# The recurrent mixer's projections in another order, four buffers of split weights, gating scale and bias on VectorE, second output factor inside the solve

## What is computed

```python
p = rmsnorm(x, ev_norm) @ ev_w_in            # columns: u 512, va 512, r 512, k 512, v 512, lora 256
# gating half
vn = (va - mean) * rsqrt(var + eps) * ln_g + ln_b
y_a = u * (einsum('gts,bnsgc->bntgc', w_s * causal, vn) + b_s)
# recurrent half: r, k, v, lora parts are mixed with the row before
p = p + (shift_prev(p) - p) * mu
w, a, g = decay(lw), sigmoid(a0 + la @ a2), sigmoid(lg) @ g2
kk = normalised(k * k_k);  k = k * (1 + (a - 1) * k_a)
S = S * w + (S @ -kk) (kk * a)^T + v k^T;  o = S @ r      # over 256 steps
out = (norm(o) * gn_g + gn_b + sum(r * k * r_k) * v) * g
x = x + concat(y_a, out) @ ev_w_out
```

## Time and profile before

| | us |
|---|---|
| median of three runs | 1414.9 (1414.65 to 1417.06) |
| the profiled execution | 1414.84 |
| its span | 1413.0 |
| mean granted clock of TensorE | 0.976 |

### The profile page before, as it was taken

One profiled execution on the slowest core, in us unless ns is written; L12 is line 12 of the kernel. 1 busy time (PEld: TensorE's weight loads), 2 busy tenths in 40 slices (PEclk: granted clock), 3 DMA queues, 4 the chain that ended last, 5 costly groups with the idle time before them and its releaser, 6 DMA issues.

```text
span 1413.0 us, 24106 instructions
## 1 busy us (share of the span) xinstructions
PE 1333.2 (94%) x10315; PEld 1211.0 (86%) x10315; DVE 955.3 (68%) x1237; ACT 684.2 (48%) x974; POOL 22.6 (2%) x30
## 2 busy tenths in 40 slices
...
GB/s 292 142 119 61 4 120 209 238 239 239 241 177 180 178 61 60 265 194 262 252 248 135 177 122 119 60 350 328 339 305 260 132 224 179 123 208 198 188 179 60
DMA packets 161284, 263.78 MB, mean 187 GB/s; under 512 B 3533, under 2 KB 95897, under 8 KB 161178
## 3 DMA queue, kind: packets, MB, share of 16 engines
...
## 4 chain that ended last, share of the span: by engine, by line
PE 74%; DVE 12%; ACT 7%; issue 5%; DMA 2%; POOL 0%; SPq 0%; DVEq 0%; ACTq 0%; POOLq 0%
PE ps L867 22%; PE ps L840 13%; PE ps L841 13%; PE ps L842 13%; ACT whi L522 2%; PE ps L1968 2%; DVE wlo L528 2%; DVE acc L1846 2%; DMA ring<-in_ff_w_up_dram 1%; PE ps L2264 1%; DVE arena L1793 1%; PE ps L853 1%; PE ps L854 1%; PE ps L855 1%; DVE arena L1814 1%
## 5 line engine op out<-in xcount | busy, mean ns | idle before, releaser
L528 DVE TENSOR_TENSOR wlo<-ring,whi 128x2048 fp32r<-128x2048 f32 x195 | 445.6, 2289 | 227.4 <-ACT whi L522 227.1
L840 PE MATMUL ps<-ghi,whi 128*128 128x256 f32 x1856 | 521.9, 281 | 9.0 <-DVE glo L776 6.9
L841 PE MATMUL ps<-glo,whi 128*128 128x256 f32 x1856 | 517.6, 279 | 0.0
L842 PE MATMUL ps<-ghi,wlo 128*128 128x256 f32 x1856 | 517.1, 279 | 0.0
L522 ACT ACTIVATE whi<-ring 128x2048 fp32r<-128x2048 f32 x195 | 370.9, 1911 | 87.6 <-PE ps L867 68.0
L840 PEld LDWEIGHTS ps<-ghi,whi 128*128 128x128 f32 x1856 | 348.6, 188 | 15.8 <-issue 12.8
L841 PEld LDWEIGHTS ps<-glo,whi 128*128 128x128 f32 x1856 | 347.9, 187 | 1.0 <-issue 0.7
L842 PEld LDWEIGHTS ps<-ghi,wlo 128*128 128x128 f32 x1856 | 348.2, 188 | 0.0
L867 PE MATMUL ps<-whi,yhi 128*128 128x512 f32 x480 | 154.7, 404 | 5.0 <-DVE wlo L528 3.7
L867 PE MATMUL ps<-wlo,yhi 128*128 128x512 f32 x480 | 150.4, 395 | 0.0
L867 PE MATMUL ps<-whi,ylo 128*128 128x512 f32 x480 | 149.8, 394 | 0.0
...
## 6 DMA issues: line engine op xcount, KB each, us to landing
...
```

What stands on the lines that cost most here:

```text
L528: e.tensor_tensor(shaped(WLO[i % NB], k), v, shaped(WHI[i % NB], k).bitcast(F32), ALU.subtract).then_inc(S["w_lo"], 1)
L840: e.matmul(o, wh, h[0][:, k, :], start=k == 0, stop=False)
L841: e.matmul(o, wh, h[1][:, k, :], start=False, stop=False)
L842: x = e.matmul(o, wl, h[0][:, k, :], start=False, stop=k == NK - 1)
```

## The change

Five parts. The projections' order is `lora`, `k`, `va`, `r`, `u`, `v`; the banks' order and the queues of all five engines follow. `NB` is 4 and every stream is one half further ahead; a scratch area that nothing uses is made smaller for it. The gating half's gain and bias move from GpSimd to VectorE, into two fused operations per half that take the place of one; the gating's bias is one product of 512 columns per bank in place of one per block. `P2` moves into the second round of the solve. The column transposes and `rk` sums lie between `v 0` and `v 1`.

```diff
@@ -19,7 +19,7 @@
 NF = FF // 128
 NS = 2
 SLOT = 4096
-NB = 3
+NB = 4
 HALF = 2048
 KAPPA = float(np.exp(-0.5))
...
     w_in = A["ev_w_in"][0]
     chunks.append(("lora", cols_of(w_in, [2560], 256)))
-    for name, s in (("k", 1536), ("r", 1024), ("v", 2048), ("va", 512), ("u", 0)):
+    for name, s in (("k", 1536), ("va", 512), ("r", 1024), ("u", 0), ("v", 2048)):
         chunks.append((name, cols_of(w_in, [s], 512)))
     add_out("ev_out", A["ev_w_out"][0])
...
@@ -249,13 +249,11 @@
     r = Ring(range(6))
     P.use(("col", 6), r())
     norm(0, r, False)
-    for key in [("col", 0), ("lora", 0), ("k", 0), ("k", 1), *(("sg", w, q) for q, w in TWO), ("r", 0),
-                ("nm", 0), ("nm", 1), ("g", 0), ("g", 1), ("r", 1), ("v", 0), ("v", 1),
-                *(("col", t) for t in range(1, 6))]:
-        P.use(key, r())
     P.use(("va", 0), 6)
     P.use(("va", 1), 7)
-    for key in [("rk", 0), ("rk", 1), ("vt", 0), ("vt", 1), "ws", ("u", 0), ("ya", 0), ("ya", 1), ("u", 1)]:
+    for key in [("col", 0), ("lora", 0), ("k", 0), ("k", 1), *(("sg", w, q) for q, w in TWO), ("nm", 0), ("nm", 1),
+                ("g", 0), ("g", 1), ("r", 0), ("r", 1), "ws", ("u", 0), ("ya", 0), ("ya", 1), ("u", 1), ("v", 0),
+                *(("col", t) for t in range(1, 6)), ("rk", 0), ("rk", 1), ("v", 1), ("vt", 0), ("vt", 1)]:
         P.use(key, r())
     r = Ring(range(8))
...
@@ -500,13 +498,15 @@
             for off, k, w, src in chunks[n][1]:
                 e.dma_start(c3(ring[n % NS][:, off:off + k * w], k), src).then_inc(S[f"ring{n % NS}"], 16)
+        AHEAD = NB - 1
+
         class Stream:
             def __init__(self):
                 self.made, self.taken = 0, 0
-            def go(self, ahead=2):
+            def go(self, ahead=NB - 1):
                 self.taken += 1
...
@@ -1018,14 +1018,7 @@
             for n in range(2):
                 eye(flat64(Yb[1][n]), S["y_eye"])
-            e.wait_ge(S["ln_in"], 64)
-            for n in range(2):
-                e.wait_ge(*read_out(("va", n)))
-                e.tensor_tensor(VN[n], VN[n], LNG, ALU.mult).then_inc(S["vn_gain"], 1)
-                e.wait_ge(S["vn_gain"], n + 1)
-                e.tensor_tensor(VN[n], VN[n], LNB, ALU.add).then_inc(S["vn"], 1)
-
-            e.wait_ge(*used_up("u", 1))
+            e.wait_ge(*used_up("v", 1))
             for x in AKm:
...
             exps((0, 1))
             exps((2, 3))
+            for q in range(2):
+                t = TMP[:, 2 * q:2 * q + 2, :]
+                e.wait_ge(*read_out(("nm", q)))
+                e.activation(t, t, ACT.Ln).then_inc(S["kk_log"], 1)
+                e.wait_ge(S["kk_log"], q + 1)
+                e.activation(t, t, ACT.Exp, scale=-0.5).then_inc(S["kk_rstd"], 1)
             split_hi(e, w.go())
-            mixed(5)
+            for q in range(2):
+                e.wait_ge(S["g_mm"], q + 1)
+                for a in range(2):
+                    j = 2 * q + a
+                    ps = ps_of(("g", q))[:, 256 * a:256 * a + 256]
+                    e.activation(P1[:, j, :], ps, ACT.Copy, scale=cc("ev_gn_g", j))
+                e.activation(GATE[:, 2 * q:2 * q + 2, :], c3(ps_of(("g", q))[:, :], 2),
+                             ACT.Copy).then_inc(bank_sem(("g", q)), 1)
             e.wait_ge(S["e2"], 1)
             e.activation(E1, E2, ACT.Exp, scale=KAPPA).then_inc(S["s0_scale"], 1)
-            split_hi(e, w.go())
-            mixed(6)
-            split_hi(e, w.go())
             for n in range(2):
                 q = mv[:, 4 * n:4 * n + 4]
                 e.wait_ge(S["va_mean"], n + 1)
                 e.activation(q[:, 2:3], q[:, 1:2], ACT.Ln, bias=LN_EPS).then_inc(S["va_log"], 1)
                 e.wait_ge(S["va_log"], n + 1)
                 e.activation(q[:, 3:4], q[:, 2:3], ACT.Exp, scale=-0.5).then_inc(S["va_rstd"], 1)
-            for n in range(2):
-                e.wait_ge(S["v_turned"], n + 1)
-                e.activation(VT[:, n, :], ps_of(("vt", n))[:, :], ACT.Copy).then_inc(bank_sem(("vt", n)), 1)
+            split_hi(e, w.go())
+            mixed(3)
+            split_hi(e, w.go())
+            mixed(4)
             split_hi(e, w.go())
             for q in range(2):
                 e.wait_ge(S["ya_mm"], q + 1)
-                e.wait_ge(S["vn"], 2)
                 e.activation(MX[:, 2 * q:2 * q + 2, :], c3(ps_of(("ya", q))[:, :], 2),
                              ACT.Copy).then_inc(bank_sem(("ya", q)), 1)
             split_hi(e, w.go())
             for q in range(2):
                 e.wait_ge(*read_out(("u", q)))
                 e.activation(YT[0][:, 2 * q:2 * q + 2, :], MX[:, 2 * q:2 * q + 2, :], ACT.Copy).then_inc(S["ya_hi"], 1)
-                if q == 0:
-                    split_hi(e, w.go())
+            split_hi(e, w.go())
+            mixed(5)
+            split_hi(e, w.go())
+            mixed(6)
+            for n in range(2):
+                e.wait_ge(S["v_turned"], n + 1)
+                e.activation(VT[:, n, :], ps_of(("vt", n))[:, :], ACT.Copy).then_inc(bank_sem(("vt", n)), 1)
...
@@ -1479,6 +1468,35 @@
             x.then_inc(S["k_factor"], 1)
             e.wait_ge(S["k_factor"], 1)
             e.scalar_tensor_tensor(Km[:, :, :], TMP[:, :, :], 1.0, Km[:, :, :], ALU.add, ALU.mult).then_inc(S["k"], 1)
+            split_lo(e, w.go())
+            for n in range(2):
+                s6, q = st6[:, 6 * n:6 * n + 6], mv[:, 4 * n:4 * n + 4]
+                e.wait_ge(*used_up("va", 1))
+                e.bn_stats(s6, ps_of(("va", n))[:, :]).then_inc(S["va_stats"], 1)
+                e.wait_ge(S["va_stats"], n + 1)
+                e.bn_aggr(q[:, 0:2], s6).then_inc(S["va_mean"], 1)
+            e.tensor_tensor(Am[:, :, :], KKm[:, :, :], Am[:, :, :], ALU.mult).then_inc(S["b"], 1)
+            e.wait_ge(S["ln_in"], 64)
+            for n in range(2):
+                q, key = mv[:, 4 * n:4 * n + 4], ("va", n)
+                e.wait_ge(S["va_rstd"], n + 1)
+                e.wait_ge(S["g_mm"], 2)
+                e.scalar_tensor_tensor(VN[n], ps_of(key)[:, :], q[:, 0:1], LNG, ALU.subtract,
+                                       ALU.mult).then_inc(bank_sem(key), 1)
+                e.wait_ge(*read_out(key))
+                e.scalar_tensor_tensor(VN[n], VN[n], q[:, 3:4], LNB, ALU.mult, ALU.add).then_inc(S["vn"], 1)
+            split_lo(e, w.go())
+            e.wait_ge(S["ws_turned"], 1)
+            e.tensor_tensor(c3(WS, 4), c3(ps_of("ws")[:, :], 4), rep(CT[:, C_UI:C_UI + 128], 4),
+                            ALU.mult).then_inc(bank_sem("ws"), 1)
+            mixed(3)
+            split_lo(e, w.go())
+            e.wait_ge(S["exps"], 2)
+            e.wait_ge(S["b"], 1)
+            for x in range(2):
+                c = slice(2 * x, 2 * x + 2)
+                e.tensor_tensor(Bt[:, c], Bt[:, c], EMS[x], ALU.mult).then_inc(S["tilted"], 1)
+            e.scalar_tensor_tensor(At, At, -1.0, EP[:, :, :, 0:128], ALU.mult, ALU.mult).then_inc(S["tilted"], 1)
             mixed(4)
...
@@ -1537,11 +1511,27 @@
                 e.wait_ge(*used_up("u", q))
                 e.wait_ge(*read_out(("ya", q)))
                 e.tensor_tensor(u, u, c3(ps_of(key)[:, :], 2), ALU.mult).then_inc(bank_sem(key), 1)
+            e.wait_ge(S["rk_in"], 1)
+            for x in range(2):
+                c = slice(2 * x, 2 * x + 2)
+                e.tensor_tensor(Kt[:, c], Kt[:, c], EMS[x], ALU.mult).then_inc(S["tilted"], 1)
+            e.tensor_tensor(Rt, Rt, EP[:, :, :, 1:129], ALU.mult).then_inc(S["tilted"], 1)
+            split_lo(e, w.go())
+            for q in range(2):
+                u = MX[:, 2 * q:2 * q + 2, :]
                 e.wait_ge(S["ya_hi"], q + 1)
                 e.tensor_tensor(YT[1][:, 2 * q:2 * q + 2, :], u, YT[0][:, 2 * q:2 * q + 2, :].bitcast(F32),
                                 ALU.subtract).then_inc(S["ya_lo"], 1)
-                if q == 0:
-                    split_lo(e, w.go())
+            mixed(5)
+            split_lo(e, w.go())
+            for t in range(1, 6):
+                dve_column(e, t)
+            mixed(6)
+            for q in range(2):
+                key, v = ("rk", q), Vm[:, 2 * q:2 * q + 2, :]
+                e.wait_ge(S["rk_mm"], q + 1)
+                e.wait_ge(S["v_turned"], 2)
+                e.tensor_tensor(v, v, c3(ps_of(key)[:, :], 2), ALU.mult).then_inc(bank_sem(key), 1)
...
@@ -1579,6 +1569,13 @@
                     e.copy_predicated(Yb[(i - 1) % 2][n].rearrange("p g j c -> p (g j) c"), mask64(C_Y64 + 64 * i, 8),
                                       c3(ps_of(key)[:, :], 8)).then_inc(bank_sem(key), 1)
                 rest_out(i - 1)
+                if i == 2:
+                    for j in range(4):
+                        e.wait_ge(*read_out(("rk", j // 2)))
+                        e.wait_ge(*read_out(("g", j // 2)))
+                        x = e.scalar_tensor_tensor(P2[:, j, :], Vm[:, j, :], cc("ev_gn_b", j), GATE[:, j, :], ALU.add,
```

(52 more changed lines are left out.)

85 lines of the change are left out of this document (11 added, 74 removed).

## The result

| | before | after |
|---|---|---|
| median | 1414.78 (1412.33 to 1417.06, 4 executions) | 1395.06 (1386.56 to 1396.34, 4 executions) |
| profiled execution | 1414.84 | 1394.7 |
| its span | 1413.0 | 1392.6 |
| mean granted clock | 0.976 | 0.983 |

A forecast was written before the change was run, and what follows sets the result against it. TensorE, busy 1333.2 of 1413.0 us, was taken as the bound, with VectorE ending the first two FFNs. Mixer 20.6, less 3 for the clock, plus 6 for the FFNs: 23.6 us gain, 1391.3 us; range 1384 to 1403.

The forecast's parts named there:

- The start: Mixer entry: the split of half 3 delays ScalarE's `mixed(0)` from 26.0 to 29.8; the 3.8 us delay costs TensorE 0.7.
- `vn` in time: Before the gating products: VectorE has `vn` at 66.3, wanted at 72.2, so the 5.9 us wait goes.
- Gating: Gating products: 11.5 us at clock 0.50 become 3.6 us, taken at full clock.
- `rk`: Between the column transposes and `v 1`: new waits for `mixed(5)` and a column copy, 3.7 us in sum.
- Clock in the mixer: Around `rk` and the `v` transposes: one 3.4 us half-clock spell each, 1.7 lost each; net 3 us, bounds 0 and 9.
- a sign of being right: Solve entry: the first block near 110 to 113 us would show the prediction right.
- Rival C: Mixer: the clock stays at 1.2 GHz from the `rk` gap to the solve; gain 17.6, time 1397.3 us; chance 0.19.
- FFNs: First two FFNs: the fourth buffer gains 3 us each, 6 in all, since VectorE sets their end; bounds 2 and 10.
- Rival B: First two FFNs: TensorE bounds them, so the fourth buffer brings its whole 10 us; time 1387.3 us; chance 0.12.
- D: Buffers behind the mixer: they move waits and end nothing, 0 to 1 us for that part; time 1396.7 us; chance 0.12.
- GpSimd's `TTc` beside `v 0`: Around `v 0`: GpSimd's copy contends with VectorE's work and could make `rk 1` 0 to 1.6 us later; left to the range.
- `P2`: Solve: four VectorE operations, 1.7 us, covered by waits; unit matrix 0.7 us late for VectorE; taken as nothing, bound 0 to 1.

The follow-up runs named there:

- filled kernel: Changed kernel plus six idle products of constants in TensorE's gaps around `rk` and the `v` transposes: 1394.11 us; run again beside the changed kernel, 1391.88 us.
- short `acc`: Changed kernel with the accumulating operations of the first two FFNs 32 columns wide instead of 512, leaving part of the modulation out: 1379.28 us, ratio 0.9756.
- after's second profile: The changed kernel itself, unchanged, profiled again in a later experiment: span 1396.2 us; its run beside two others on one chip measured 1395.36 us.
- old order: Kernel before with NB = 4 and the streams one half further ahead, nothing else changed: 1410.34 us, ratio 0.9977 [0.9956, 0.9998].

## Why the prediction was right, and where it missed

- **The start held.** Half 3 lands so that its split ends at 29.9, `mixed(0)` begins at 29.8 (forecast 29.8), the squares begin at 44.5 (forecast: the first done at 45.5), a wait of 0.75 (forecast 0.7), norm to 47.3. In the other profiles in which the first call splits three halves this wait is 0.3 to 2.3 us; with three buffers, or two halves in the first call, there is none.
- **`vn` in time.** Forecast 66.3 for a want at 72.2; measured 66.2 and 72.21. The operations are 0.74 and 0.75, as estimated. The wait of 5.9 is gone.
- **Gating: 4.3 for 3.6.** The two-instruction bias product takes 1.05 from start to start, where I had 0.86 from the norm's 128-row instructions, and each group of eight instructions 1.08, where I had 0.95. A term mis-sized by 0.7. That it ran at full clock held in the first profile of after, and in part by luck: in three of the nine profiles with this form and no wait ahead of it (after's second and both of the filled kernel) the clock was down for 3.4 us from its end on.
- **`rk`: 1.50 and 2.17 for 1.2 and about 2.4.** Right in place, cause and sum (3.67 for 3.7). With the slow second `rk` product `v 1` starts at 94.2, not at 93.1.
- **Clock in the mixer: the term that was mis-sized.** The places were right, the length not in this profile. I took one spell of 3.4 us in each place, 1.7 us each. There are two of 6.8. The first costs 2.1 in `v 1` (4.2 us at half) and 0.5 in the second `rk` product; the second makes the way from the `v` transposes to the first block 11.0 us (104.07 to 115.09) where it is 9.1 with the clock up (94.98 to 104.08): 1.9. That is 4.5 for 3.4. But with the same waits both spells were 3.4 us, as forecast, in the kernels with three buffers and with the short `acc`, and 6.8 again in after's second profile. So which length came was not in the reach of the rows, and what sets it stays open. The forecast's 109.5 with 3.4 for the clock is 112.9; measured 115.1, outside the 110 to 113 that the prediction named as a sign of being right. Of these 2.2 the clock is 1.1, the gating 0.7, and 0.4 is spread over the rest. The sum's term for the clock, 3, is also 0.6 more than its own parts give (3.4 less the 1.0 of the old spell is 2.4).
- **Rival C**, half clock all the way to the solve, did not come: the clock was up for 3.5 us at the end of `v 1`, between the two stretches. Products of constants in the gaps held it up throughout (0.77 to 1.00). The Trainium skill ("TensorE: Matmul & The Clock Gate", "What's actually happening") makes activity the condition of the high level. The trace agrees here; the last part has stretches at half clock in which TensorE was busy throughout, and those this rule alone does not give.
- **FFNs: 4.4 to 4.8 for 6.** That VectorE ends them is shown by the short `acc`. The two FFNs gave 2.4 and 2.2 us in after, where 3 each was forecast, and 3.5 and 3.0 in the old order: the 3 is about right there, and the total is lower because the mixer lost 1.5. Why it is less in the new order is not shown. Rival B (10) falls by the interval of the old order, which allows 6.2 us at most. D (1 or less) falls by the traces of the FFNs; the times alone, with 0.3 to 6.2 us, don't exclude it.
- **GpSimd's `TTc` beside `v 0`: nothing of the 0 to 1.6** (its pair of copies at 88.34 took 1.63, near the 1.49 of an undisturbed pair in before, and `rk 1` waited no longer than forecast).
- **`P2`: nothing**, as forecast, with the late unit matrix where it was said to be (GpSimd's copy at 130.45, VectorE stood 2.60 us, TensorE not at all).
- The sum: 3.9 us missed, of 23.6. 2.1 in the mixer (clock 1.1 and gating 0.7 its largest parts) and 1.1 behind it (4.9 for 6); the last 0.7 is that the span of the profiled execution fell by 20.4 and the median by 19.7. That both parts came out so near is in part luck. By after's second profile the mixer misses by 5.6, and what follows the mixer took 1185.6 to 1191.1 us in the ten profiles with four buffers and nothing left out, 1192.6 in before: on one profile, anything from 1.5 to 7.0 could have stood for the 6.

What I did not see: the order that I took as given held both the `rk` waits and the clock loss behind them. `v 1` needed only another bank to run in the gap, and that was worth more, 11 us, than all that the forecast missed.

## What to carry to other kernels

Where a change closes large waits and opens small ones, price the small ones with the clock behind them, and look for work of the same engine that a mere change of bank lets run in the gap: here that was worth 11 us, against 1.0 and 3.5 in two measurements for filling it with idle products. A deeper buffer gives only what the next engine in line leaves; find that engine's last operation first. And check what a longer look-ahead pulls to the front of an in-order queue: here one early split cost the mixer 1.5 us with the old order.

## What the runs showed of the chip

**The clock fell with no gap ahead of it.** In the second profile of the filled kernel TensorE ran `r 1`, `ws`, `u 0` and the gating without a wait, and the clock was down for 3.4 us from 74.5 on, from the end of the gating into `u 1` (first row, which covers the start of it). With the bias per block it was down for 10.2 us from 75.2 on (second row, the first 6.8 of them):

```profile
72.20:76.50 4.30, 4.30 (x22) 3.42 (x23) 4.30 (x5) 1.05 (x2) 0.00 (x0) 0.77 0.65 267
```

```profile
75.20:82.00 6.80, 6.80 (x21) 5.00 (x22) 3.54 (x5) 1.63 (x3) 0.00 (x0) 0.50 0.55 192
```

The first profile of after has 1.00 there, its second 3.4 us at half clock. Why it falls in some executions and not in others stays open; no run here was made to tell.

**One kernel, two executions, other stretches.** In the dilated attention after stood at half clock for 17.1 us with TensorE fully busy; its second profile had 1.00 there, but 6.8 us at half clock in the mixer's output, where the first had none:

```profile
504.60:521.70 17.10, 17.09 (x65) 14.78 (x66) 8.36 (x16) 7.11 (x17) 0.00 (x0) 0.50 0.00 1
```

```profile
500.00:530.00 30.00, 27.86 (x166) 22.28 (x165) 19.69 (x36) 14.74 (x37) 0.00 (x0) 1.00 0.20 66
157.20:164.00 6.80, 5.38 (x68) 4.82 (x67) 0.32 (x1) 2.21 (x5) 0.00 (x0) 0.50 0.81 259
```

Ten of the thirteen profiles of this study (before and after included) have such a stretch of 13.7 to 17.1 us there. Executions of after range from 1386.56 (mean clock 0.989) to 1403.15 (0.979). A single profile's span therefore can't rank kernels that lie 5 us apart; distances between two places with the same clock between them can.

**VectorE and GpSimd take turns.** In the kernel with gain and bias on GpSimd the split that starts at 64.95 beside GpSimd's product (64.46 to 65.76) ends at 67.91: 0.81 us until that product ends, and then 2.15, about its time alone. GpSimd's addition from 65.84 ends 1.16 us after that split, again about the 1.3 of its like alone, and the second pair repeats it (70.32 to 72.46 is 2.14; 72.46 to 73.59 is 1.13). These times fit each waiting for the other's whole operation, and both lost. The Trainium skill ("SBUF — State Buffer", "Who interferes with whom") states just this for a VectorE operation with two inputs in SBUF; here the trace agrees.
